# A two-block transformer kernel on one core: the delta-rule scan's inverse in 32x32 blocks, the norms' squares moved into the stages before, three hardware loops written out

## The reference

```python
def rms_norm(x, gain=None):
    y = xf * lax.rsqrt(jnp.mean(xf * xf, axis=-1, keepdims=True) + EPS)
...
def _chunked_gated_delta(q, k, v, g, beta, s0):
    G = jnp.cumsum(g, axis=-1)
    gamma = jnp.exp(jnp.where(incl, G[..., :, None] - G[..., None, :], -jnp.inf))
    a_low = jnp.where(strict, jnp.einsum('bhnid,bhnjd->bhnij', kb, k) * gamma, 0.0)
    uw = lax.linalg.triangular_solve(eye + a_low, rhs, left_side=True, lower=True, unit_diagonal=True)
    ...
    def step(s, inp):
        v_new = u_n - jnp.einsum('bhck,bhkv->bhcv', w_n, s)
        o_n = jnp.einsum('bhck,bhkv->bhcv', qd_n, s) + jnp.einsum('bhij,bhjv->bhiv', qk_n, v_new)
        s = s * jnp.exp(gl_n)[..., None, None] + jnp.einsum('bhck,bhcv->bhkv', kd_n, v_new)
```

## Time and profile before

| | us |
|---|---|
| median of 3 runs | 4053.33 |
| lowest, highest | 4053.07, 4076.39 |
| profiled execution, its own time | 4051.13 |
| span of its trace | 4049.3 |
| TensorE busy | 3681.5 |
| DVE, ACT, POOL busy | 2007.8, 910.5, 461.2 |

### The profile page before, as it was taken

How to read it: one execution, slowest core, us unless ns; L and a number is a source line. 1 busy time by engine, 2 the same in 40 slices (tenths; PEclk the granted TensorE clock), 3 DMA queues, 4 the chain that set the end, 5 groups by cost and what they waited for, 6 DMA issues and landing times.

```text
span 4049.3 us, 54462 instructions
## 1 busy us (share of the span) xinstructions
PE 3681.5 (91%) x22980; PEld 3032.1 (75%) x22980; DVE 2007.8 (50%) x2777; ACT 910.5 (22%) x1583; POOL 461.2 (11%) x374
## 2 busy tenths in 40 slices
PE   5989999989899999889988999899999799969996
PEld 3777677767776778678877887688887577658885
DVE  3455333544453335656655665532235652765346
ACT  1124100221231002334433442110011201721011
POOL 0001000000010000006610661030000100512000
PEclk9879999988799999999998999899999899989998
DMA  3210444322104442210011003111111211012222
GB/s 132 83 63 12 154 166 176 116 85 83 53 22 164 168 178 102 99 42 3 2 38 43 2 2 132 61 53 63 63 63 68 85 63 63 1 52 84 94 94 83
DMA packets 48615, 314.44 MB, mean 78 GB/s; under 512 B 5836, under 2 KB 6732, under 8 KB 13944
## 3 DMA queue, kind: packets, MB, share of 16 engines
q1 hardware_dynamic: 37440, 272.65, 18.5%
q10 hardware_dynamic: 10936, 38.31, 2.5%
HBM read 301.38 MB, written 9.56 MB: 77 GB/s over the span
## 4 chain that ended last, share of the span: by engine, by line
PE 78%; DVE 8%; DMA 6%; issue 2%; ACT 2%; PEld 2%; POOL 1%; POOLq 0%; ACTq 0%; PEldq 0%; DVEq 0%; SPq 0%; another core or an unknown queue 0%
PE psum L511 19%; PE psum L513 18%; PE psum L512 18%; DMA pieces_in<-pieces 5%; PE psum L2101 4%; PE psum L2111 3%; PE psum L2099 2%; DVE pieces_lo L536 1%; PE psum L1156 1%; PE psum L2931 1%; PE psum L1129 1%; PE psum L1140 1%; PE psum L2953 1%; PE psum L643 1%; DVE pieces_hi L529 1%
## 5 line engine op out<-in xcount | busy, mean ns | idle before, releaser
L511 PE MATMUL psum<-xt_operands,pieces_hi 128*128 128x512 f32 (+1 forms) x2544 | 945.3, 372 | 30.6 <-DVE pieces_lo L536 25.6
L512 PE MATMUL psum<-xt_operands,pieces_hi 128*128 128x512 f32 (+1 forms) x2544 | 928.3, 365 | 0.0
L513 PE MATMUL psum<-xt_operands,pieces_lo 128*128 128x512 f32 (+1 forms) x2544 | 928.1, 365 | 0.0
L511 PEld LDWEIGHTS psum<-xt_operands,pieces_hi 128*128 128x128 f32 x2544 | 481.5, 189 | 149.3 <-issue 41.2
L529 DVE CAST pieces_hi<-pieces_in 128x2048 fp32r<-128x2048 f32 x206 | 257.3, 1249 | 575.9 <-DMA pieces_in<-pieces 490.2
L513 PEld LDWEIGHTS psum<-xt_operands,pieces_lo 128*128 128x128 f32 x2544 | 481.0, 189 | 78.0
L512 PEld LDWEIGHTS psum<-xt_operands,pieces_hi 128*128 128x128 f32 x2544 | 481.8, 189 | 75.3 <-issue 2.4
L536 DVE TENSOR_TENSOR pieces_lo<-pieces_in,pieces_hi 128x2048 fp32r<-128x2048 f32 x206 | 480.1, 2331 | 5.7
L511 PE MATMUL psum<-pieces_hi,xt_operands 128*128 128x512 f32 (+1 forms) x1000 | 404.7, 405 | 31.0 <-DVE pieces_lo L536 17.9
L512 PE MATMUL psum<-pieces_lo,xt_operands 128*128 128x512 f32 (+1 forms) x1000 | 391.8, 392 | 0.0
L513 PE MATMUL psum<-pieces_hi,xt_operands 128*128 128x512 f32 (+1 forms) x1000 | 391.7, 392 | 0.0
(11 more groups left out here) (323 smaller groups left out, 4771.8 us busy)
## 6 DMA issues: line engine op xcount, KB each, us to landing
pieces_in<-pieces SPq DMA_DIRECT2D x260, 1024.0 KB, 4.8
arena<-mods ACTq DMA_DIRECT2D x8, 512.0 KB, 14.3
arena<-ln ACTq DMA_DIRECT2D x4, 1024.0 KB, 4.6
x_park<-x_mem ACTq DMA_DIRECT2D x1, 3072.0 KB, 11.3
o_park<-arena ACTq DMA_DIRECT2D x2, 1536.0 KB, 5.4
arena<-o_park ACTq DMA_DIRECT2D x1, 3072.0 KB
x_mem<-x_park ACTq DMA_DIRECT2D x1, 3072.0 KB, 18.0
arena<-line ACTq DMA_DIRECT2D x6, 448.0 KB, 6.1
```

Of the source, the lines that this page charges most:

```text
L511: signal_later(k, pe.matmul(out, sh, mh, start=start, stop=False))
L512: signal_later(k, pe.matmul(out, sh, ml, start=False, stop=False))
L513: return pe.matmul(out, sl, mh, start=False, stop=stop)
```

## The change

**Scan.** The inverse is made in the four 32x32 diagonal blocks of each 128x128 matrix, and such a set is stored 32 columns wide (128 partitions by 4 heads by 32). `ul` takes `low`'s diagonal blocks and their turned copies by products with a 32x32 identity. `a1` and `a2` form the squares of the block and of its turned copy at once (two sets each), `a3` the last one. `x2`, `x4`, `x8` stay as powers, 32 wide. `wy` makes the turned inverse and the masked product, `xx0` the product of these in the wide layout, `z0` its turned form. `y1`, `xx1` and then `w2`, `y2`, `xx2` join to 64 and 128; these read `low` itself, so that POOL's masking is gone. `gb` turns the stored prefix sums in place of a product with a triangular mask. `dlow` and `s1` go from DVE to POOL. The bank rings become seven banks and one, and all four orders are new.

**Norms.** The squares, the root and the inversion move to the end of the stage before (`squares_act`, `squares_dve`): setup, `out` and `ffn1`. The wait for the small parameters moves behind the scaled rows. It also runs at the end of the last `ffn1`, where nobody reads it.

**Loops.** The hardware loops over layers and halves become written-out loops on the four compute engines; SP's loop over pieces stays. DVE's wait for the parked `x` has a semaphore of its own (`x_parked`), so that it does not wait for the parked output of the first half.

```diff
-    ("b16", 128), ("level", 384)
+    ("b16", 32), ("corner16", 32), ("eye", 32), ("zero_eye", 64)
...
-            with pe.Fori(0, DEPTH):
+            for _layer in range(DEPTH):
...
-    with e.eng.Fori(0, 2) as k.half:
+    for k.half in range(2):
...
+def squares_act(k, e, spare, added=None):
+    for t in range(NT1):
+        if added:
+            act.wait_ge(added, NT1 + t + 1)
+        if t:
+            act.wait_ge(S.squares_ready, t)
+        act.activation(spare, k.x1[:, t, :], ACT.Square, accum_out=k.small[:, t:t + 1]).then_inc(S.squares_ready, 1)
+    act.wait_ge(S.meansq_ready, 1)
+    act.activation(k.small[:, 12:16], k.small[:, 8:12], ACT.Sqrt).then_inc(S.std_ready, 1)
...
 def rms_act(k, e, name, turn):
+    if name == "attn_norm":
+        act.wait_ge(S.loaded, 16)
...
 def out_act(k, e, _):
     turn_scaled_act(k, e, (k.x1h, k.x1l), ROWS_TURN[NT1])
     cond_act(k, e, _)
+    squares_act(k, e, k.back_x[:, 0:D], S.mm_taken)
...
+    "pe": order("z0.1' xx0.1' xx1.0' o1.0' y1.1' w2.0' y2.0' xx1.1' gb.0 xx2.0' w2.1' y2.1' o1.1' xx2.1' vn.0' vn.1' "
+      "o2.0' gb.1 o2.1' su.1' su.0' kk.0 kk.1 qk.0 qk.1 ul.0 ks.1 a1.0 ul.1 a2.0 x2.0 a1.1 a3.0 x4.0 a2.1 "
+      "x2.1 x8.0 a3.1 x4.1 wy.0 x8.1 ks.0 xx0.0 wy.1 z0.0 y1.0 "),
...
-RING_BANKS = 4
+RINGS = ((1, 7), (0, 1))
...
+BLOCKS = tuple(slice(32 * n, 32 * n + 32) for n in range(4))
+    def blocks(out, lhs, rhs):
+        for h in range(HALF):
+            for r in BLOCKS:
+                last = pe.matmul(out[r, h, :], lhs(h, r), rhs(h, r), start=True, stop=True)
+        return last
...
+    def gb(s, d):
+        product(s, d, "gb", prefixes, None)
+    def ul(s, d):
+        for h in range(HALF):
+            for r in BLOCKS:
+                pe.matmul(out[r, 0, h, :], low[r, h, r], eye[r, :], start=True, stop=True)
+        for r in BLOCKS:
+            last = pe.matmul(out[r, 1, :, :], eye[r, :], low[r, :, r], start=True, stop=True)
+    def square(s, d, name, src, *needs):
+        blocks(out[:, 1, :, :], of(d, src, 0), of(d, src, 1))
+        st.done(blocks(out[:, 0, :, :], of(d, src, 1), of(d, src, 0)))
+    def wy(s, d):
+        blocks(out[:, 0, :, :], of(d, "xc"), lambda h, r: eye[r, :])
+        st.done(blocks(out[:, 1, :, :], of(d, "lv"), of(d, "xc")))
+    def y1(s, d):
+        for h in range(HALF):
+            for rows, others in quarters(d):
+                last = pe.matmul(small(k, "y1", s, d)[rows, h, :], low[others, h, rows], x[others, h, others], start=True, stop=True)
...
-    def ut(s, d):
-    def l2(s, d):
-    def u2(s, d):
-    def l4(s, d):
-    def u4(s, d):
-    def l8(s, d):
-    def w0(s, d):
-    def w1(s, d):
-    def y0(s, d):
...
-    def ld(s, d):
-    def lv0(s, d):
-    def lv1(s, d):
-    def lv2(s, d):
```

More of the change, by code:

```diff
@@ L2102, in product, with of @@
         st.done(last)
[L2104 to L2108, removed]
+    def blocks(out, lhs, rhs):
         for h in range(HALF):
[L2110 to L2124, removed]
+            for r in BLOCKS:
+                last = pe.matmul(out[r, h, :], lhs(h, r), rhs(h, r), start=True, stop=True)
+        return last
+    def of(d, name, a=None):
+        return lambda h, r: k.buf[d][name][r, h, :] if a is None else k.buf[d][name][r, a, h, :]
     def x(s, d, h):
@@ L2180, in w1 @@
[L2180 to L2199 removed]
+        single(s, d, "x8", of(d, "l8"), of(d, "xc"), "l8c", "x4a")
@@ new lines, in wy, with xx0 @@
+    def wy(s, d):
+        if not runs(s):
+            return
+        ready(s, d, "wy", ("x8a",))
+        out = small2(k, "wy", s, d)
+        blocks(out[:, 0, :, :], of(d, "xc"), lambda h, r: eye[r, :])
+        st.done(blocks(out[:, 1, :, :], of(d, "lv"), of(d, "xc")))
+    def xx0(s, d):
+        if not runs(s):
+            return
+        ready(s, d, "xx0", ("wya",))
+        for h in range(HALF):
+            for r in BLOCKS:
+                last = pe.matmul(bank(k, "xx0", s, d)[r, h, r], k.buf[d]["wy"][r, 0, h, :], k.buf[d]["wy"][r, 1, h, :],
+                                 start=True, stop=True)
+        st.done(last)
@@ new lines, in z0 @@
+    def z0(s, d):
+        single(s, d, "z0", of(d, "wy", 1), of(d, "wy", 0), "wya")
+    def y1(s, d):
+        if not runs(s):
+            return
+        ready(s, d, "y1", ("xf",))
+        low, x = low_of(k, s, d), x_of(k, s, d)
+        for h in range(HALF):
+            for rows, others in quarters(d):
+                last = pe.matmul(small(k, "y1", s, d)[rows, h, :], low[others, h, rows], x[others, h, others],
+                                 start=True, stop=True)
+        st.done(last)
@@ new lines, in xx1, with corner @@
+    def xx1(s, d):
+        if not runs(s):
+            return
+        ready(s, d, "xx1", ("y1c",))
+        for h in range(HALF):
+            for rows, _ in quarters(d):
+                last = pe.matmul(small(k, "xx1", s, d)[rows, h, :], k.buf[d]["z0"][rows, h, :], k.buf[d]["y1"][rows, h, :],
+                                 start=True, stop=True)
+        st.done(last)
+    def corner(s, d, name, lhs, rhs, *needs):
+        if not runs(s):
+            return
+        ready(s, d, name, needs)
+        rows, _ = halves(d)
+        for h in range(HALF):
+            last = pe.matmul(middle(k, name, s, d)[rows, h, :], lhs(h), rhs(h), start=True, stop=True)
+        st.done(last)
@@ L3061, in second_pe @@
         stage_end(k, e, "pe")
-    with e.eng.Fori(0, 2):
+    for _half in range(2):
         for f, _, _, _, arg in PER_HALF:
```

308 lines of the change are left out of this document (173 added, 135 removed).

## The result

| | us |
|---|---|
| changed kernel, median of 4 | 4104.53 (4101.16 to 4104.95) |
| kernel before, median of 4 beside it | 4053.94 (4053.07 to 4076.39) |
| ratio | 1.0115, 95% interval 1.0093 to 1.0137 |
| profiled execution of the changed kernel: own time, span | 4104.15, 4102.2 |

The account below looks back on a forecast made before the run. TensorE's queue was taken to bound the scan turn; 24.2 us of work, 2.0 for shapes and 2.1 of waits gave 28.3 for 37.55. Both scans -111 us, norms and loops -16: 3926 us, range 3890 to 4005.

Parts of the forecast that it names:

- Narrow operations: In the scan, sixteen 32x32 products take 0.25 us on TensorE, with all four tiles running at once.
- TensorE's work: In one scan turn, TensorE's operations sum to 24.2 us, and changes of tile shape add 2.0.
- The other engines: In one scan turn, DVE at 17.4 us, POOL at 17 and ACT below 12 don't take over from TensorE.
- Waits: In one scan turn, TensorE waits 2.1 us, bounds 1 and 4, for chains of short steps and slow first instructions.
- Rival 1: In the scan, four tiles aren't filled, sixteen small products take 0.47 us; 33.2 us a turn, kernel 3985 us; 17%.
- Rival 2: In the scan, the clock halves in the narrow stretch: +9.8 us a turn, kernel 4044 us; 10%.
- Rival 3: In the scan, matmul starts average 29 ns apart over all tiles: 44.9 us a turn, kernel 4124 us; 7%.
- Norms and loops: Outside the scan, earlier norms and written-out loops give -15.8 us, from -20 to -6.
- Rival 4: Outside the scan, norms and loops give nothing because transfers are due first: 3942 us; counted with the main case.

Follow-up runs that it names:

- filler: The changed kernel with one unread 128x128 matmul of 256 columns behind each set of sixteen 32x32 products of `blocks`; 4087.07 us, ratio 1.0076.
- spread: The changed kernel's same operations and instruction count in other orders, one direction's narrow products between the other's whole ones; 3994.44 us, ratio 0.9847.
- probe: The changed kernel with six stretches of unread, unwaiting matmuls in 64x64, 32x32 and 128x128 tiles ahead of each half's scan; 4597.73 us.
- one_pass: The changed kernel with 32x32 products, except in `ul`, `y1` and `xx1`, reading operands as bfloat16, one matmul each instead of two; 4001.61 us, ratio 0.9860.
- norms_loops: The kernel before with the change's norms part, written-out loops and separate wait for the parked `x`, scan untouched; 4040.72 us, ratio 0.9958.
- norms_only: The kernel before with the change's norms part alone, hardware loops and single semaphore kept; 4049.29 us, ratio 0.9984.

## Why the prediction was wrong

The forecast went by a sum of durations, and at the full clock the durations were right. Point by point:

- **Narrow operations, 0.25 us for sixteen products**: right, 0.25 to 0.28 at the full clock. Four tiles run at once.
- **TensorE's work, 24.2 us and 2.0 for shapes**: right; filler leaves 25.6.
- **The other engines**: right. DVE 17.1 (17.4 forecast), POOL 15.3 (17), ACT 10.9 (below 12).
- **Waits, 2.1 us, from 1 to 4**: this step failed. I asked what each narrow operation waits for, and never how fast instructions arrive. The idle time was 8.8 us a turn, all of it ended by "issue" and none by DVE or ACT: the instruction supply. With it came the half clock, by the two estimates 7 to 10 us more. The forecast's work and shapes, the idle time and a remainder of 9.3 for the clock, 26.2 + 8.8 + 9.3, give the 44.3.
- **Rival 1** named the loading of instructions, as a slower feed of the tiles, and dropped most of its chance because of the earlier trace rows. Those rows show three starts at once, and so that the queue can start tiles together when its instructions are there. They cannot show how many come in a microsecond. The row that could was in hand, in the earlier trace rows: 186 packets, for 2 x 22980 instructions by the page of the kernel before, 247 each. With 1080 matmuls a turn the count alone gives 8.4 packets in 28.3 us, one in 3.4 us, where the turn of before needs 1062 instructions in 37.55 us, 4.1 packets, one in 9. No row showed that 3.4 us can be had, and the range should have held a price for it.
- **Rival 2** (the clock) came true as a part. The price per turn was 9.8 us, the measured one 7 to 10 by estimate, but that the two agree is in part luck: the price was put on the narrow products and the two `ks`, and over half of the loss by the second estimate is whole products and corners. Nor was it independent: the clock stayed at 0.92 to 0.99 with the same narrow products once they were spread (spread) or filled up (filler), so narrowness alone doesn't bring the half clock, and neither do the pauses alone (the probe's 64 columns, 0.96). It was low where 32-column products and idle time came together. In one_pass, with one or two such pauses a turn and half as many narrow instructions, the granted clock was 0.71 all the same; how much of that is the pauses and how much the waits between the shorter operations was not taken apart.
- **Rival 3** gave 44.9 us a turn and 4124 us, close to the measured 44.3 and 4104.5, by another mechanism. Starts are 8 to 9 ns apart within a group at the full clock and 13 at the half, not 29; 3.5 us for 128 matmuls is 27 ns in the mean. The Trainium skill ("TensorE: Matmul & The Clock Gate", section on the 56 ns gap) has a floor of about 25 ns between starts. With tiles the probe's starts within a group contradict it, 128 in 1.1 us, and only the mean over groups comes near it. Whether that floor holds for a single tile no run here shows.
- **Norms and loops, -15.8 us**: -17 in norms_loops. TensorE started at 55.63 (55.2 forecast), layer 0 to 1 left 11.4 us idle (12), the first half's end 1.57 (1.3). `out` to `ffn1` gained 1.4 (1.3): in layer 0 TensorE's products lay 3.0 us earlier than before ahead of it and 4.4 behind it (4.7 once both were at the full clock). The end of layer 1 cost 1.6 to 2.2, not 4.8 (11.2 ahead, 9.6 at the first product behind, 9.0 later). Rival 4, that these parts give nothing, fell.

Summed up: 4053.9 + 68 for the scans - 17 = 4105.

## What to carry to other kernels

Beside the busy time of a plan, count its instructions: here TensorE got 256 (weight loads and matmuls alike) in some 3.3 to 3.5 us at best, so a longer stretch that used 256 in less stopped at the end of each group, however short its matmuls were. Smaller tiles saved TensorE's time here (0.25 us for sixteen 32x32 products, 0.47 for eight of 64x64) and cost instructions (2160 a turn for 1062); mix them with wide work, so that no group is narrow throughout, and merge products that share a stationary operand. Look for "issue" as the releaser in the middle of an operation, and for equal counts between the pauses. And test a resource by its rate over microseconds, not by one burst that the queue had already in hand.

## What the runs showed of the hardware

- A float32 product in 32x32 tiles costs about the same with 32, 64 and 128 columns if it stands among its like: 56.3, 58.9 and 59.4 us for 1024. With 32 and 64 columns that is the instruction supply (27 and 23 us idle); with 128 it is TensorE's own work (57.7 us busy), which happens to be as long.
- The first pause behind the scan's whole products was anything from 0.33 to 1.99 us over ten turns of the changed kernel; the later ones were 1.42 to 2.52, but for one of 0.44.
- The granted clock over the probe's three 32x32 stretches was 0.55, 0.90 and 1.00. The first two had a pause of 1.5 to 2.3 and mostly 1.5 to 1.8 us at nearly every group's end, the third two pauses in all, of 1.16 and 0.32.
- The hardware loops saved no packets: with the same 22980 matmuls, norms_only (with loops) has 186 packets of q8 and norms_loops (written out) 182.
- The stage `nsa` of the first block, untouched by all of this, takes 81.1 us at a clock of 0.92 or 86.6 to 88.6 at 0.83 to 0.85. Before, and in norms_loops, both layers had 81.1; in the changed kernel layer 0 had 86.6 and layer 1 81.1. That is why its first scan began only 9.4 us earlier and that of norms_loops 14.9. The profiled execution of norms_only had some 88.6 us in both layers. The stage's code is the same in all of them; what decides is open, and differences of some us between kernels outside the scan have to be read with this in mind:

```profile
286.59:373.17 86.58, 86.58 (x576) 67.69 (x576) 45.79 (x213) 42.68 (x109) 11.43 (x26) 0.85 0.01 1
1080.18:1161.30 81.12, 81.11 (x576) 63.88 (x576) 45.87 (x213) 42.53 (x109) 11.44 (x26) 0.92 0.00 1
```
